# Fewer visits between the weight products: indexer in four, levels in five, sample scores in one, mask and bias in fp32r

## What is computed

```python
# indexer: 16 heads of 64; k_sel = 64 (prompt), 65 (samples, keys 256 past + 4 new)
s = einsum('bthd,bld->bthl', qi, ki) * 64 ** -0.5
scores = einsum('bth,bthl->btl', wi * 16 ** -0.5, relu(s))
idx = top_k(where(admissible, scores, -inf), k_sel)
logits = einsum(q, k[idx]) * 128 ** -0.5 + rel_bias[bucket(t - idx)]
o = softmax(where(valid, logits, -1e30)) @ v[idx]
# gated linear attention: decay exp(b_t - b_s) inside causal chunks, log_a = log_sigmoid(gate) / 16
att = einsum('bthk,bshk,btshk->bhts', q, k, exp(b[:, :, None] - b[:, None, :]))
```

## Time and profile before

| | |
|---|---|
| median of three runs | 1417.62 us (1417.62 to 1417.71) |
| profiled execution | 1417.78 us |
| its span, first to last instruction | 1416.1 us |
| PE busy | 1401.9 us (99%) |
| DVE busy | 846.8 us (60%) |
| ACT busy | 583.6 us (41%) |
| POOL busy | 114.0 us (8%) |
| input projection, halves 0 to 81 | 10.0 to 349.1 us |

### The profile page before, as it was taken

How to read it: one execution, slowest core, us unless ns; L and a number is a source line. 1 busy time by engine, 2 the same in 40 slices (tenths; PEclk the granted TensorE clock), 3 DMA queues, 4 the chain that set the end, 5 groups by cost and what they waited for, 6 DMA issues and landing times.

```text
span 1416.1 us, 28410 instructions
## 1 busy us (share of the span) xinstructions
PE 1401.9 (99%) x10636; PEld 1378.2 (97%) x10636; DVE 846.8 (60%) x1173; ACT 583.6 (41%) x708; POOL 114.0 (8%) x170
## 2 busy tenths in 40 slices
PE   7999999999999999999999999999999999999998
PEld 7989998999999999999999999999999999999998
DVE  6668865756876555555554444555555556666554
ACT  6455653366333433333333333333333333335332
POOL 2223103200222000000000000000000001111000
PEclk9999999999999999999999999999999999999999
DMA  8746534445645454545555556545454545556553
GB/s 302 200 149 207 171 120 138 144 143 177 207 159 171 160 171 161 165 161 167 163 142 164 164 165 192 167 159 170 160 166 159 172 130 163 163 163 200 171 164 116
DMA packets 75767, 236.66 MB, mean 167 GB/s; under 512 B 13696, under 2 KB 14352, under 8 KB 75336
## 3 DMA queue, kind: packets, MB, share of 16 engines
q1 hardware_dynamic: 71136, 223.59, 49.8%
q0 software_dynamic: 3696, 11.51, 2.7%
q10 hardware_dynamic: 888, 0.93, 0.2%
HBM read 231.44 MB, written 4.47 MB: 167 GB/s over the span
## 4 chain that ended last, share of the span: by engine, by line
PE 98%; ACT 1%; DVE 0%; DMA 0%; issue 0%; SPq 0%; DVEq 0%; ACTq 0%
PE acc L473 31%; PE acc L475 31%; PE acc L474 31%; PE px L1545 1%; PE px L1435 0%; PE px L1514 0%; PE px L1495 0%; ACT rl_s L744 0%; DMA proj<-in_xT 0%; PE px L473 0%; PE px L475 0%; PE px L474 0%; PE px L1611 0%; PE px L1507 0%; PE px L1593 0%
## 5 line engine op out<-in xcount | busy, mean ns | idle before, releaser
L439 DVE TENSOR_TENSOR w_lo<-w_raw,w_hi 128x1024 fp32r<-128x1024 f32 (+2 forms) x448 | 508.0, 1138 | 316.9 <-ACT w_hi L433 308.0
L433 ACT ACTIVATE w_hi<-w_raw 128x1024 fp32r<-128x1024 f32 (+2 forms) x448 | 441.5, 989 | 546.6 <-PE acc L475 538.6
L473 PE MATMUL acc<-n_hi,w_hi 128*128 128x288 f32 x1664 | 492.8, 296 | 0.0
L474 PE MATMUL acc<-n_lo,w_hi 128*128 128x288 f32 x1664 | 490.9, 295 | 0.0
L475 PE MATMUL acc<-n_hi,w_lo 128*128 128x288 f32 x1664 | 489.2, 294 | 0.0
L475 PEld LDWEIGHTS acc<-n_hi,w_lo 128*128 128x128 f32 x1664 | 313.5, 188 | 0.0
L474 PEld LDWEIGHTS acc<-n_lo,w_hi 128*128 128x128 f32 x1664 | 312.4, 188 | 0.1
L473 PEld LDWEIGHTS acc<-n_hi,w_hi 128*128 128x128 f32 x1664 | 311.8, 187 | 0.1
L473 PE MATMUL acc<-x_hi,w_hi 128*128 128x288 f32 x848 | 258.1, 304 | 10.0 <-DVE w_lo L967 10.0
L474 PE MATMUL acc<-x_lo,w_hi 128*128 128x288 f32 x848 | 251.4, 297 | 0.0
L475 PE MATMUL acc<-x_hi,w_lo 128*128 128x288 f32 x848 | 250.6, 296 | 0.0
(11 more groups left out here) (271 smaller groups left out, 829.2 us busy)
## 6 DMA issues: line engine op xcount, KB each, us to landing
w_raw<-in_w_gu SPq DMA_DIRECT2D x176, 512.0 KB, 4.0
w_raw<-in_w_in SPq DMA_DIRECT2D x78, 512.0 KB, 4.0
w_raw<-in_w_down SPq DMA_DIRECT2D x64, 384.0 KB, 3.1
w_raw<-in_w_down SPq DMA_DIRECT2D x64, 320.0 KB, 3.0
w_raw<-in_w_ple SPq DMA_DIRECT2D x32, 576.0 KB, 3.8
w_raw<-in_w_out SPq DMA_DIRECT2D x32, 512.0 KB, 4.6
proj<-in_xT SPq DMA_DIRECT2D x4, 576.0 KB, 6.3
w_raw<-in_w_in SPq DMA_DIRECT2D x8, 256.0 KB, 5.0
```

What stands on the lines that cost most here:

```text
L433: nc.scalar.activation(whi[:, slot, 0:kt * P], raw[:, slot, 0:kt * P], ACT.Copy).then_inc(S("w_hi_done"), 1)
L439: nc.vector.tensor_tensor(wlo[:, slot, 0:kt * P], raw[:, slot, 0:kt * P], whi[:, slot, 0:kt * P].bitcast(F32), ALU.subtract).then_inc(S("w ...
L473: nc.tensor.matmul(out, w_h, row_of(m_hi_, k0 + k), start=first and k == 0, stop=False)
L474: nc.tensor.matmul(out, w_h, row_of(m_lo_, k0 + k), start=False, stop=False)
```

## The change

- **Indexer.** `index` q = 0 to 3 does both prompt tiles of a pair of head rows in one visit (halves 9, 11, 14, 18): tile 0 in banks 4 and 5, tile 1 in banks 0 and 1. `rl` becomes two buffers. ACT takes two relus, DVE sums both.
- **Sample scores.** All eight samples in one visit (half 20), into banks 2 to 5: both row halves of a sample now write one bank, in different partitions. One relu of 128x1152 on ACT. The four sums over heads (half 22) go to four column groups of bank 2, without accumulation; each holds two samples' scores, so that `sc_s` has 128 rows and `ex` picks from each group its own samples.
- **Mask and bias in fp32r.** `ex` and `eb` are copied to fp32r on ACT at the start, the choice is written as fp32r by DVE (`chosen_s`, at the place of `sc_s`), the bias is split in two fp32r parts on POOL (rows 0 to 31 and 32 to 63 of `bias_r`). Both matmuls have 128 rows. POOL reads the bias twice.
- **Levels.** `level` v = 0 to 4 does levels (0), (1, 2), (3, 4), (5, 6), (7, 8) in halves 53, 55, 57, 60, 63; even levels in banks 4 and 5. Each engine does the pair's work in one stage. `vb_nat` also waits for `level_read` 5.
- **ScalarE's gate.** ACT's part of `gate` becomes the stage `softplus`, in half 25.

The diff, cut to its core (DVE's sums of `index` run over both tiles as ACT's relus do):

```diff
     9: [("bias_out", 0), ("index", 0)],
-    10: [("index", 1)],
-    11: [("index", 2)],
-    12: [("index", 3)],
-    14: [("index", 4)],
-    15: [("index", 5)],
-    18: [("index", 6), ("keys_i", 0)],
-    19: [("index", 7)],
-    20: [("index_s", 0), ("index_s", 1), ("pick", (0, 0, 2))],
-    21: [("norm_sq", 0), ("index_s", 2), ("index_s", 3), ("pick", (0, 2, 4))],
-    22: [("norm", 0), ("index_s", 4), ("index_s", 5), ("pick", (0, 4, 6))],
-    23: [("index_s", 6), ("index_s", 7), ("pick", (0, 6, 8))],
-    24: [("index_end", 0), ("gate", 0), ("pick", (1, 0, 1))],
-    25: [("pick", (1, 1, 3))],
+    11: [("index", 1)],
+    14: [("index", 2)],
+    18: [("index", 3), ("keys_i", 0)],
+    20: [("index_s", 0), ("pick", (0, 0, 2))],
+    21: [("norm_sq", 0), ("pick", (0, 2, 4))],
+    22: [("norm", 0), ("index_end", 0), ("pick", (0, 4, 6))],
+    23: [("pick", (0, 6, 8))],
+    24: [("gate", 0), ("pick", (1, 0, 1))],
+    25: [("softplus", 0), ("pick", (1, 1, 3))],
     26: [("pick", (1, 3, 5))],
     27: [("values", 0), ("store_kv", 0), ("pick", (1, 5, 7))],
     28: [("pick", (1, 7, 8)), ("pick_s", (0, 1))],
...
     52: [("mix", 3), ("mix_s_back", 0), ("decays", 0)],
     53: [("transpose_s", 1), ("level", 0)],
     55: [("mix_s", 1), ("level", 1)],
-    56: [("mix_s_back", 1), ("level", 2)],
-    57: [("level", 3)],
-    58: [("level", 4)],
+    56: [("mix_s_back", 1)],
+    57: [("level", 2)],
     59: [("vb_nat", 0)],
-    60: [("level", 5)],
-    61: [("level", 6)],
-    63: [("level", 7)],
-    64: [("last", 0), ("level", 8)],
+    60: [("level", 3)],
+    63: [("level", 4)],
...
     rb, rt, rh = np.arange(P) // 32, np.arange(P) % 32 // NH, np.arange(P) % NH
-    put("ex", np.stack([(b[:, None] == (4 * x + rb)[None, :]) & (i[:, None] == rt[None, :])
+    pb, pi, own = p % TS // NS, p % NS, p // TS == p % TS // (2 * NS)
+    put("ex", np.stack([own[:, None] & (pb[:, None] == (4 * x + rb)[None, :]) & (pi[:, None] == rt[None, :])
                         for x in range(2)], 1) * BIG)
-    put("eb", np.arange(32)[:, None] == (rt * NH + rh)[None, :])
+    put("eb", (p[:, None] < 2 * TS) & (p[:, None] % TS == (rt * NH + rh)[None, :]))
...
+        choice_r = beneath("choice_r", [P, 3 * P])
...
+        chosen_s = beneath("chosen_s", [P, T])
...
+        def index_bank(tt):
+
+            return 0 if tt else 4
+
+        def level_bank(m):
+
+            return 4 if m and m % 2 == 0 else 0
+
+        VISITS = [(0,), (1, 2), (3, 4), (5, 6), (7, 8)]
...
-            read_bias(bias_s[:, 0:PAST], DMAX - PAST, NS, PAST)
-            read_bias(bias_n[:, :], DMAX, NS, NS)
+            pool.wait_ge(S("att_zero"), 1)
+            for p0 in (0, TS):
+                read_bias(bias_s[p0:p0 + TS, 0:PAST], DMAX - PAST, NS, PAST)
+                read_bias(bias_n[p0:p0 + TS, :], DMAX, NS, NS)
...
+            pool.wait_ge(S("bias_loaded"), 16 * (P // NCOPY + 4))
+            two, low = slice(0, 2 * TS), slice(TS, 2 * TS)
+            link(nc.gpsimd.tensor_copy(bias_s[two, PAST:T].rearrange("p (b i) -> p b i", b=NB),
+                                       bias_n[:, :].unsqueeze(1).broadcast_to([2 * TS, NB, NS])))
+            link(nc.gpsimd.tensor_copy(prob_s[two, :].bitcast(F32R), bias_s[two, :]))
+            link(nc.gpsimd.tensor_tensor(bias_r[low, :], bias_s[low, :], prob_s[low, :], ALU.subtract))
+            link(nc.gpsimd.tensor_copy(bias_r[0:TS, :], bias_s[0:TS, :]))
+            nc.gpsimd.tensor_copy(bias_r[2 * TS:P, :], bias_s[2 * TS:P, :]).then_inc(S("bias_split"), 1)
+            pool.wait_ge(S("bias_split"), 1)
...
+            act.wait_ge(S("consts_loaded"), 32)
+            A(choice_r[:, :], consts[:, 0:3 * P], ACT.Copy).then_inc(S("choice_ready"), 1)
...
-            def index(n):
-
-                nk = P * (n % 2 + 1)
-                act.wait_ge(S("idx_mm"), n + 1)
-                if n:
-                    act.wait_ge(S("rl_free"), n)
-                src = px[:, 0:2, :].rearrange("p e (j s) -> p e j s", j=2)[:, :, :, 0:nk]
-                dst = rl[:, :, :].rearrange("p (e j) s -> p e j s", e=2)[:, :, :, 0:nk]
-                A(dst, src, ACT.Relu).then_inc(S("relu_done"), 1)
-
-            def index_s(b):
-
-                act.wait_ge(S("idx_s_mm"), b + 1)
-                if b >= 4:
-                    act.wait_ge(S("idx_s_acc"), b // 2 - 1)
-                for e in range(2):
-                    at = 64 * (b % 2) + 32 * e
-                    A(rl_s[at:at + 32, b // 2 % 2, :], px[at:at + 32, 4 + e, 0:T], ACT.Relu).then_inc(S("relu_s_done"), 1)
+            def index(q):
+
+                act.wait_ge(S("idx_mm"), q + 1)
+                for tt in range(2):
+                    if q:
+                        act.wait_ge(S("rl_free"), 2 * q - 1 + tt)
+                    bank = index_bank(tt)
+                    src = px[:, bank:bank + 2, :].rearrange("p e (j s) -> p e j s", j=2)[:, :, :, 0:P * (tt + 1)]
+                    A(rl[tt][:, :, :].rearrange("p (e j) s -> p e j s", e=2), src, ACT.Relu).then_inc(S("relu_done"), 1)
+
+            def index_s(_):
+
+                act.wait_ge(S("idx_s_mm"), 1)
+                A(rl_s[:, :, :], px[:, 2:6, 0:T], ACT.Relu).then_inc(S("relu_s_done"), 1)
...
-            def level(m):
-                if m + 1 < 8:
-                    decays(m + 1)
+            def level(v):
+                for m in (() if v == 4 else (1,) if v == 0 else (2 * v, 2 * v + 1)):
+                    decays(m)
...
-                dve.wait_ge(S("idx_s_acc"), NB // 2)
-                V.tensor_copy(sc_s[:, 0:T], px[0:TS, 2, 0:T]).then_inc(S("sc_s_read"), 1)
+                dve.wait_ge(S("idx_s_acc"), 1)
+                V.tensor_copy(sc_s[:, 0:T], px[:, 2, 0:T]).then_inc(S("sc_s_read"), 1)
...
-                    V.tensor_scalar(sc_s[:, 0:T], sc_s[:, 0:T], MARK, -1.0, ALU.not_equal, ALU.mult)\
+                    V.tensor_scalar(chosen_s[:, :], sc_s[:, 0:T], MARK, -1.0, ALU.not_equal, ALU.mult)\
...
-            def level(m):
-
-
-                dve.wait_ge(S("level_mm"), m + 1)
-                if m == 0:
+            def level(v):
+
+
+                dve.wait_ge(S("level_mm"), v + 1)
+                if v == 0:
                     dve.wait_ge(S("att_zero"), 1)
-                if m == 1:
-                    V.tensor_copy(att_c[:, :, :, :], px[:, 0:2, 0:256].rearrange("p e (r t) -> p e r t", r=2))\
-                        .then_inc(S("level_read"), 1)
-                else:
-                    mask = C["ident"] if m == 0 else C["lev"][:, (m - 2) * P:(m - 1) * P]
-                    V.copy_predicated(att[:, :, :, :], mask.bitcast(U32).unsqueeze(1).unsqueeze(1).broadcast_to([P, 2, 4, P]),
-                                      px[:, 0:2, :].rearrange("p e (a t) -> p e a t", a=4)).then_inc(S("level_read"), 1)
-                    dve.wait_ge(S("level_read"), m + 1)
-                if m < 8:
+                for m in VISITS[v]:
+                    bank = level_bank(m)
+                    if m == 1:
+                        V.tensor_copy(att_c[:, :, :, :], px[:, bank:bank + 2, 0:256].rearrange("p e (r t) -> p e r t", r=2))\
+                            .then_inc(S("level_read"), 1)
+                    else:
+                        mask = C["ident"] if m == 0 else C["lev"][:, (m - 2) * P:(m - 1) * P]
+                        V.copy_predicated(att[:, :, :, :], mask.bitcast(U32).unsqueeze(1).unsqueeze(1).broadcast_to([P, 2, 4, P]),
+                                          px[:, bank:bank + 2, :].rearrange("p e (a t) -> p e a t", a=4)).then_inc(S("level_read"), 1)
+                        dve.wait_ge(S("level_read"), m + 1)
+                for m in (() if v == 4 else (2 * v, 2 * v + 1)):
...
-                    pe.wait_ge(S("relu_done"), n)
-                for jj in range(2):
+                if q:
+                    pe.wait_ge(S("relu_done"), 2 * q)
+                for tt in range(2):
+                    nk, bank = P * (tt + 1), index_bank(tt)
+                    for jj in range(2):
+                        for e in range(2):
+                            pp = slice(64 * e, 64 * e + 64)
+                            ins = M(px[:, bank + e, 256 * jj:256 * jj + nk],
+                                    proj[pp, ROW_QI + 2 * q + jj, P * tt:P * tt + P], proj[pp, ROW_KI if e else ROW_KD, 0:nk],
+                                    start=True, stop=True)
+                ins.then_inc(S("idx_mm"), 1)
+
+            def index_end(_):
+
+                pe.wait_ge(S("relu_s_done"), 1)
+                pe.wait_ge(S("btab_ready"), 1)
+                for pair in range(NB // 2):
+                    ins = M(px[TS * pair:TS * pair + TS, 2, 0:T], wb[:, pair, :], rl_s[:, pair, :], start=True, stop=True)
+                ins.then_inc(S("idx_s_acc"), 1)
+
+            def index_s(_):
+                pe.wait_ge(S("keys_i_done"), 1)
+                pe.wait_ge(S("relu_done"), 8)
+                pe.wait_ge(S("ki_pages"), 16 * NPG * NB)
+                for b in range(NB):
```

(52 more changed lines are left out.)

99 lines of the change are left out of this document (39 added, 60 removed).

## The result

The changed kernel takes **1408.86 us** (median of four runs, 1408.58 to 1409.1) against 1417.62 for the kernel before: a ratio of 0.9938, 95% interval 0.9921 to 0.9956, so 8.8 us less. The forecast was 1409.1. Its profiled execution took 1408.88 us.

What follows compares the result with a forecast made beforehand. TensorE's work list bounds the kernel (busy 1401.9 of 1416.1 us). Savings of 1.6 + 3.9 + 1.5 + 1.4 = 8.4, brought to 8.5, take 1417.62 to 1409.1 us; 8-in-10 range 1407.7 to 1411.8.

Steps and rivals of the forecast that it cites:

- Indexer: Input projection, eight indexer visits merged to four: 4 merges at 0.39 us each save 1.6 us.
- Samples: Sample scores in one visit, head sums in four column groups: net saving 3.9 us, between 2.5 and 4.2.
- bank and column groups: Sample visit: row halves share one bank at once (2.06 us, else 4.0); sums in four column groups side by side (0.62).
- Choice and bias: Mask and bias matmuls of the sample logits in fp32r with 128 rows: saves 1.5 us (1.3 to 1.7).
- Levels: Nine level visits merged to five: saves 1.4 us (1.2 to 1.6).
- the pair (1, 2): Merging levels 1 and 2 saves the fixed 0.19 us and little else, since half 56 keeps its visit.
- The sum: All four terms: 8.4 us, brought to 8.5 for borders rounded down; bounds all one way, 6.5 or 9.4.
- Off TensorE: Added work on ACT, POOL and DVE (constants' copy, bias, levels) stays hidden: 0 us.
- The thinnest cover: DVE's sq_lo, awaited by norm at the end of half 22: 0.5 us of room left, so 0 us.
- 1 us for 1 if it is gone: Once the room of sq_lo is used up, each us of lateness costs 1 us.
- rival (a): Covers too thin near half 33: 3.5 us given back, 1412.6; milder, sq_lo late, 1410 to 1411; chance 0.17.
- The softplus: Moving it to half 25 removes DVE's 3.63 us idle gap; room at half 33, 2.0 us, grows a little.

Runs made afterwards that it cites:

- e5: Kernel before the change with only ScalarE's softplus moved from half 24 to 25: 1417.68 us, ratio 0.9999.
- e3: Changed kernel with ScalarE's softplus put back in half 24: 1411.17 us, ratio 0.996.
- e6: Changed kernel with the wide sample relu on ACT done twice: 1409.57 us.
- e7: Changed kernel with the wide sample relu on ACT done three times: 1412.38 us.
- e1: Changed kernel with the indexer put back into eight visits: 1410.39 us, ratio 0.9949.
- e10: Changed kernel with the two row halves of the sample scores writing different banks (picks differ): span 1406.9 us, score visit 2.07 us against 2.08.
- e8: Changed kernel with the samples' four head sums accumulated in rows 0 to 31, one column group: 1410.41 us, ratio 0.9947.
- e4: Changed kernel with the mask and bias matmuls in plain fp32, the 128 rows kept: 1410.28 us, ratio 0.9949.
- e2: Changed kernel with the levels put back into nine visits: 1410.40 us, ratio 0.9949.
- e13: Changed kernel with the wide sample relu on ACT done four times: median 1413.66 us of ten runs, ratio 0.9974.
- e12: Changed kernel with the indexer in eight visits and the softplus back in half 24: 1412.78 us, ratio 0.9966.

## Why the prediction was right

**What bounds the kernel**: shown. Every edit on TensorE's list moved the time by its length, and the edit elsewhere (e5) by 0.1 us at most, up to the point where a cover ends (e3, e6, e7).

**Indexer** 1.6, measured 1.55; the visits of 1.5 us came as forecast. The cover had one near limit that the text did not see, the key transfer (0.2 us in e1).

**Samples** 3.9, measured 3.94, with 2.08 us for the visit (forecast 2.06) and 0.62 for the sums. The two questions in it, bank and column groups, went the way that the earlier trace rows said; e10 and e8 show each by itself. That the sum fits to 0.04 us is in part luck: the halves that lost their visits gave 0.47 us (13.81 to 13.01 for the four, less the stall of 0.33) where I had 0.38, and the gate 0.11 (0.86 to 0.75) where I had 0.19.

**Choice and bias** 1.5, measured 1.60; e4 splits it in 1.4 for the passes and 0.2 for the 128 rows, the upper end of the forecast's 0.1 to 0.2.

**Levels** 1.4, measured 1.56. The term for the pair (1, 2) was mis-sized: I gave it the fixed 0.2 alone. In e2 the two matmuls of the back-transpose last 0.31 us from start to start ahead of a level; in the changed kernel, alone in half 56, they last 0.14. That is the missing 0.17.

**The sum.** The terms add up to 8.4 without rounding too (1.56 + 3.94 + 1.5 + 1.36), so the step from 8.4 to 8.5 had nothing behind it. Their bounds add up to savings of 6.6 and 9.1 us, not 6.5 and 9.4. Measured were 8.65 for the four terms and 0.26 beside them.

**Off TensorE.** The constants' copy, POOL's bias work and the levels on DVE cost nothing, as said. The thinnest cover, sq_lo of norm 0, has 0.46 us left where I wrote 0.5, and "1 us for 1 if it is gone" held in e6 but not beyond: from 1.8 us on the clock can fall and double the price. My rival (a) had the wait alone in its price: its hard form, 3.5 us late, would probably have been dearer for that reason (e13's 3.0 us were, in eight of ten runs). For its mild form, up to 1.5 us late, that isn't shown, as no run has a wait between 0.7 and 1.8.

**The softplus** was judged right in effect and wrong in place. I argued from w_lo of half 33, whose room would "grow a little"; it grew from 2.0 to 3.4, and even with the softplus in half 24 it is 1.9. The cover that needed the move is sq_lo of norm 1, with 0.27 us of room before, which the prediction doesn't name. It also held DVE's times against TensorE's 5.5 us of gain, indexer and samples alike; e12 shows that the indexer's share costs no room there, and the traces that the samples' share does. That last is read from the traces and has no run of its own.

**No version beats the changed kernel**: each part undone costs its term, and none of the runs points to a waste that is left on TensorE's list.

## What to carry to other kernels

When one engine is busy for 99%, cost a change by that engine's list, start to start: here four terms from eight rows gave the saving to 0.4 us of 8.9. Then list every wait of that engine behind the changed place, not only the one for weights, and note its room; a move that is worth nothing alone (e5) can be what lets the rest through (e3). Whether a room shrinks depends on what opens the late engine's queue: a gain ahead of that event is free, one behind it is not. And price a wait of TensorE above its length once it comes near 2 us: here one of 1.8 us cost 2.0 to 4.1 us (e3).

## What was not expected of the hardware

- The granted clock can fall to one half after an idle stretch of 1.8 us in a kernel that is otherwise 99% busy; it fell about 1 us after TensorE had resumed, stayed for 3 to 4 us and cost some 1.6 us more (e7, e12). It doesn't fall in every execution: with 3.0 us of idling the profiled one kept its full clock, two of ten runs took the wait alone, and four took 3.0 us more (e13).
- Four 32-column matmuls in four column groups of one bank take 0.62 us where the same four, one after the other, take 2.06 (e8), and two row halves in one bank cost nothing (e10).
